# Two 32-row expert blocks per pass through the array instead of one, in a two-layer hybrid backbone with a grouped mixture of experts

## The reference

```python
D_MODEL, N_EXPERTS, TOP_K, EXPERT_FF = 1024, 16, 2, 512

def swiglu(x, wg, wu, wd):
    return (jax.nn.silu(x @ wg) * (x @ wu)) @ wd

def moe(v, router_w, router_bias, w_gate, w_up, w_down, s_gate, s_up, s_down):
    ...
    out = swiglu(xt, s_gate, s_up, s_down)
    for e in range(N_EXPERTS):
        out = out + gates[:, e:e + 1] * swiglu(xt, w_gate[e], w_up[e], w_down[e])
    return out.reshape(B, T, D)
```

## Time and profile before

| | |
|---|---|
| median of the three runs | 2375.11 us (2373.59 to 2384.86) |
| profiled execution, first to last instruction | 2369.5 us |
| profiled execution's own time | not listed apart; the median lies 5.6 us above its span |
| expert blocks of layer 0 | 772.1 to 1126.4 us, 354.3 us |
| expert blocks of layer 1 | 2059.8 to 2345.5 us, 285.7 us |
| TensorE matmul busy, whole span | 1976.5 us (83%) |
| DMA, mean over the span | 161 GB/s |

### The profile page before, as it was taken

One profiled execution on the slowest core, in us unless ns is written; L12 is line 12 of the kernel. 1 busy time (PEld: TensorE's weight loads), 2 busy tenths in 40 slices (PEclk: granted clock), 3 DMA queues, 4 the chain that ended last, 5 costly groups with the idle time before them and its releaser, 6 DMA issues. The chain is left out here.

```text
span 2369.5 us, 58411 instructions
## 1 busy us (share of the span) xinstructions
PE 1976.5 (83%) x26021; PEld 1357.2 (57%) x26021; DVE 951.9 (40%) x1675; ACT 701.9 (30%) x1524; POOL 331.0 (14%) x211
## 2 busy tenths in 40 slices
PE   6999998998989788889396897678888887967775
PEld 3777765446744344445243783678888855634333
DVE  3184244783051111111434774666676552211112
ACT  3234543763230000000314223545544222000001
POOL 1443400003310000000110541311122000000000
PEclk8999998998989899989698997899999978988888
DMA  8544525004374897977520300000000025999984
GB/s 301 196 178 167 189 107 200 14 1 142 108 274 165 312 340 269 343 250 273 164 97 27 107 27 1 3 4 4 4 4 4 4 92 173 323 381 348 343 316 177
DMA packets 184017, 381.14 MB, mean 161 GB/s; under 512 B 14394, under 2 KB 43670, under 8 KB 183510
## 3 DMA queue, kind: packets, MB, share of 16 engines
q1 hardware_dynamic: 165216, 343.82, 40.7%
q10 hardware_dynamic: 15094, 20.99, 2.9%
q0 software_dynamic: 3456, 12.58, 1.4%
HBM read 634.54 MB, written 25.95 MB: 279 GB/s over the span
## 5 line engine op out<-in xcount | busy, mean ns | idle before, releaser
L1810 PE MATMUL banks<-arena 128*32 128x256 f32 x1696 | 234.1, 424 | 94.6 <-DMA arena<-in_exp_w_up_dram 94.6
L369 PE MATMUL banks<-parts 128*128 128x512 f32 (+1 forms) x1096 | 243.9, 375 | 22.1 <-DVE parts L383 11.3
L1811 PE MATMUL banks<-arena 128*32 128x256 f32 x1696 | 234.1, 424 | 0.0
L369 PEld LDWEIGHTS banks<-parts 128*128 128x128 f32 x1096 | 195.2, 193 | 59.4 <-DVE parts L383 11.5
L1810 PEld LDWEIGHTS banks<-arena 128*32 128x32 f32 x1696 | 105.5, 120 | 184.4 <-DMA arena<-in_exp_w_up_dram 102.9
L377 DVE TENSOR_TENSOR arena<-banks,arena 64x256 f32<-64x256 f32 (+3 forms) x128 | 65.5, 512 | 339.3 <-ACT arena L1876 244.5
L2559 PE MATMUL banks<-arena 64*64 64x64 f32 x4224 | 159.5, 225 | 49.5 <-DVE arena L380 19.2
L1876 ACT ACTIVATE arena<-banks 64x256 f32<-64x256 f32 x78 | 29.7, 381 | 573.3 <-PE banks L1811 573.3
L2559 PEld LDWEIGHTS banks<-arena 64*64 64x64 f32 x4224 | 148.2, 140 | 53.0 <-DVE arena L380 20.5
L2559 PE MATMUL banks<-ring 64*64 64x64 f32 x4224 | 159.2, 225 | 8.0 <-issue 7.8
L369 PE MATMUL banks<-arena,ring 128*128 128x256 f32 (+1 forms) x528 | 156.5, 459 | 8.5 <-PEq L316 8.5
(11 more groups left out here) (368 smaller groups left out, 3601.9 us busy)
## 6 DMA issues: line engine op xcount, KB each, us to landing
arena<-in_exp_w_gate_dram SPq DMA_DIRECT2D x106, 1024.0 KB
arena<-in_exp_w_up_dram SPq DMA_DIRECT2D x106, 1024.0 KB
arena<-in_exp_w_down_dram SPq DMA_DIRECT2D x53, 2048.0 KB
ring<-in_exp_w_gate_dram SPq DMA_DIRECT2D x50, 1024.0 KB
ring<-in_exp_w_up_dram SPq DMA_DIRECT2D x50, 1024.0 KB
ring<-in_exp_w_down_dram SPq DMA_DIRECT2D x25, 2048.0 KB
ring<-in_w_mod_dram SPq DMA_DIRECT2D x24, 2048.0 KB, 9.1
ring<-in_ab_w_in_dram SPq DMA_DIRECT2D x10, 2048.0 KB, 13.9
```

Source lines behind the costliest of these rows:

```text
L369: m = nc.tensor.matmul(o, a, b, start=first and n == 0, stop=last and n == len(pairs) - 1)
L1810: nc.tensor.matmul(o[r:r + BLOCK, 0:256], x, up[:, k, c], start=k == 0, stop=k == KD - 1)
L1811: m = nc.tensor.matmul(o[64 + r:64 + r + BLOCK, 0:256], x, gate[:, k, c], start=k == 0, stop=k == KD - 1)
```

## The change

The step of the engines becomes a pair of blocks, g = (2g, 2g+1); the last pair of each layer has one block, since 47 and 31 are odd. The four column groups of `gate_up` now hold up and gate of two blocks, 512 columns wide, and those of `down` the two halves of two blocks. Silu, multiply and copies take both blocks at once. SyncE still walks through single blocks in its old order, but what it waits for are the labels of pairs. There are still three places for weights.

```diff
-                    sp.wait_ge(*at(("first half", i - 3)))
+                    sp.wait_ge(*at(("first half", (i - 3) // 2)))
                     load_half(i, 0, expert, cond=new)
-                    sp.wait_ge(*at(("gate up", i - 3)))
+                    sp.wait_ge(*at(("gate up", (i - 3) // 2)))
                     load_half(i, 1, expert, cond=new)
                     if i > 3:
-                        sp.wait_ge(*at(("down", i - 4)))
+                        sp.wait_ge(*at(("down", (i - 4) // 2)))
                         load_down(i - 1, before, cond=before_new)
...
-                for i in range(nb + 1):
-                    if i < nb:
-                        gate_up(i, 0)
...
+                for g in range(ng + 1):
+                    if g < ng:
+                        gate_up(g, 0)
+                    if g > 0:
+                        turn_hidden(g - 1)
+                    if g < ng:
+                        gate_up(g, 1)
+                    if g + 1 < ng:
+                        turn_x(g + 1)
+                    if g > 0:
+                        down(g - 1)
...
-                pe.wait_ge(half_landed[part][p], 32 * (w0[p] + i // 3 + 1))
+                for i in blocks_of(g):
+                    pe.wait_ge(half_landed[part][i % 3], 32 * (w0[i % 3] + i // 3 + 1))
...
                 for k in range(4 * part, 4 * part + 4):
+                    for i in blocks_of(g):
+                        side = i % 2
+                        x = m_xt[:, g % 2, k, BLOCK * side:BLOCK * side + BLOCK]
+                        for first_row, w in ((0, expert_weights(i % 3, 1)), (64, expert_weights(i % 3, 0))):
+                            r = first_row + BLOCK * side
+                            m = nc.tensor.matmul(o[r:r + BLOCK, :], x, w[:, k, :], start=k == 0, stop=k == KD - 1)
...
 # down
+                for k in range(4):
+                    for i in blocks_of(g):
+                        x = m_th[:, g % 2, k, BLOCK * (i % 2):BLOCK * (i % 2) + BLOCK]
+                        for half in range(2):
+                            r = 64 * (i % 2) + BLOCK * half
+                            m = nc.tensor.matmul(ps[3 + g % 2][r:r + BLOCK, :], x, expert_weights(i % 3, 2)[:, k, 512 * half:512 * half + 512],
+                                                 start=k == 0, stop=k == 3)
```

More of the change, by code:

```diff
@@ L1593, in moe_block @@
             ng = (nb + 1) // 2
[L1594 to L1595 removed]
+            x0, w0, stored_before = x_pairs_before[0], list(loads_before), list(stores_before)
             x_pairs_before[0] += ng
@@ L1598, in moe_block, with blocks_of @@
                 loads_before[p] += in_place[p]
+            def blocks_of(g):
+                return range(2 * g, min(2 * g + 2, nb))
+            for g in range(ng):
+                stores_before[g % 2] += 16 * len(blocks_of(g))
+            stored_after = list(stores_before)
             def block_of(i):
@@ L1806, in gate_up @@
                 for k in range(4 * part, 4 * part + 4):
[L1807 to L1811, removed]
@@ L1812, in gate_up @@
-                m.then_inc(pe_done, pe.tick(("gate up" if part else "first half", i)))
-            def turn_hidden(i):
-                pe.wait_ge(*at(("hidden", i)))
-                pe.wait_ge(*at(("shared out", 2 * nt - 1)))
[L1817 to L1820, removed]
@@ new lines, in gate_up, with turn_hidden @@
+                m.then_inc(pe_done, pe.tick(("gate up" if part else "first half", g)))
+            def turn_hidden(g):
+                r = BLOCK * len(blocks_of(g))
+                pe.wait_ge(*at(("hidden", g)))
+                pe.wait_ge(*at(("shared out", 2 * nt - 1)))
+                pe.wait_ge(*at(("hidden out", g - 1)))
+                for c in range(4):
+                    m = nc.tensor.transpose(ps[2][:, c * 64:c * 64 + r], m_hid[0:r, c * P:(c + 1) * P], ident[0:r, 0:r])
+                m.then_inc(pe_done, pe.tick(("hidden turned", g)))
@@ new lines, in down @@
+            def down(g):
+                pe.wait_ge(*at(("hidden out", g)))
+                pe.wait_ge(*at(("y out", g - 2)))
+                for i in blocks_of(g):
+                    pe.wait_ge(down_landed[i % 3], 16 * (w0[i % 3] + i // 3 + 1))
+                for k in range(4):
+                    for i in blocks_of(g):
+                        x = m_th[:, g % 2, k, BLOCK * (i % 2):BLOCK * (i % 2) + BLOCK]
[3 more added lines that the diff above has]
+                                                 start=k == 0, stop=k == 3)
+                m.then_inc(pe_done, pe.tick(("down", g)))
@@ L1869, in act_ @@
                 load_x(2)
[L1870 to L1883, removed]
+                for g in range(ng + 2):
+                    if g >= 2:
+                        store_y(g - 2)
+                    if g < ng:
+                        r = BLOCK * len(blocks_of(g))
+                        act.wait_ge(*at(("gate up", g)))
+                        act.wait_ge(*at(("hidden", g - 1)))
+                        nc.scalar.activation(m_sil[0:r, :], ps[g % 2][64:64 + r, :], ACT.Silu).then_inc(act_done, act.tick(("silu", g)))
+                    if g + 1 < ng:
+                        x_out(g + 1)
+                        if g + 3 < ng:
+                            load_x(g + 3)
+                    if l == 1 and g - 1 in turns_at:
+                        j = turns_at.index(g - 1)
                         act.wait_ge(*at(("h turned", j)))
@@ L1986, in dve_ @@
                     nc.vector.tensor_copy(m_ysh[:, d // 2, 512 * (d % 2):512 * (d % 2) + 512], ps[2 + d % 5]).then_inc(dve_done, dve.tick(("shared out", d)))
[L1987 to L2001, removed]
@@ new lines, in dve_ @@
+                for g in range(ng + 1):
+                    if g > 0:
+                        dve.wait_ge(*at(("hidden turned", g - 1)))
+                        dve.wait_ge(*at(("down", g - 3)))
+                        r = BLOCK * len(blocks_of(g - 1))
+                        nc.vector.tensor_copy(m_th[:, (g - 1) % 2, :, 0:r], ps[2][:, 0:256].rearrange("p (c t) -> p c t", c=4)[:, :, 0:r]).then_inc(
+                            dve_done, dve.tick(("hidden out", g - 1)))
+                    if g < ng:
+                        r = BLOCK * len(blocks_of(g))
+                        dve.wait_ge(*at(("silu", g)))
+                        dve.wait_ge(*at(("hidden turned", g - 1)))
+                        vmul(m_hid[0:r, :], ps[g % 2][0:r, :], m_sil[0:r, :]).then_inc(dve_done, dve.tick(("hidden", g)))
+                    if g > 0:
+                        r = 64 * len(blocks_of(g - 1))
+                        dve.wait_ge(*at(("down", g - 1)))
+                        if g >= 3:
+                            dve.wait_ge(y_stored[(g - 1) % 2], stored_before[(g - 1) % 2] + 32 * (g // 2 - (g % 2 == 0)))
+                        nc.vector.tensor_copy(m_yout[0:r, (g - 1) % 2, :], ps[3 + (g - 1) % 2][0:r, :]).then_inc(dve_done, dve.tick(("y out", g - 1)))
```

62 lines of the change are left out of this document (21 added, 41 removed).

## The result

The changed kernel takes **2556.02 us** (median of 4 runs, 2552.03 to 2558.84) against 2374.45 us before: ratio 1.0767, 95% interval 1.0736 to 1.0797, so 182 us slower. Slower was right; 2470 us was 86 us short, and the time lies above the range.

A forecast was written before the change was run, and what follows sets the result against it. Neither TensorE nor DMA was the whole bound; what decided was how early loads are issued against when TensorE wants them. Waits and half clock added 69 us in layer 0 and 26 in layer 1: 2375.1 + 95 = 2470 us, range 2430 to 2520.

The forecast's parts named there:

- An odd load ... 9.1 us as median: Expert stretches: odd block's first half issued 1.7 us late, then 9.1 us to land, 10.8 us waited in all.
- Second halves: Expert stretches: waits for second weight halves, mostly behind odd loads, 2 us each or 0.8 where DMA's queue is full.
- Even loads are hidden: Expert stretches: even blocks' loads are issued one pair, 13.7 us, ahead, so they stay hidden as before.
- Nothing else moved by more than 2: Windows outside the two layers' expert stretches: none moves by more than 2 us.
- A bubble without any load, 2.0 us: Pairs without loads: TensorE waits 2.0 us for SyncE's skipped loads, most of it two register reads.
- A real down load in front, 3.0: SyncE before a pair's first half: issuing a real down load adds 1.1 us to the bubble, 3.0 in all.
- The clock ... 1.7 per wait: TensorE behind each wait of 2.8 us or more: half clock costs 1.7 us more; none behind 2.0 us bubbles.
- Rival 1: TensorE's clock falls at each bubble too: +26 to +40 us, 2500 us; chance 0.20.
- The matmuls gain: nothing: TensorE's expert matmuls: time follows columns, not the number of matmuls, so pairing blocks gains zero.
- rival 3: Gate and up are bound by the array's issue: at 50 ns saved per record, 2280 us; chance 0.03.
- rival 4: 512-column matmuls in four groups run one after another, each half four times as long: hundreds of us more; chance 0.01.
- Rival 2: SyncE's order does not bind, so loads hide better: 2350 or less in full, 2410 in half; chance 0.07.

The follow-up runs named there:

- e3: Changed kernel with y stores spread over 16 DMA engines and SyncE issuing the next blocks' gate and up loads before its wait for down: 2358.02 us.

## Why the prediction was wrong, point by point

The waits of the changed kernel, by kind, against the terms of the sum, with the same kernel with spread stores (e1) beside them. Each is the sum of TensorE's gaps over what they are without waits:

| us | predicted | changed | stores spread |
|---|---|---|---|
| layer 0: six odd loads | 74.6 | 102.6 | 75.8 |
| other pairs' first waits | 37 | 39.7 | 33.9 |
| second halves | 12 | 15.0 | 4.9 |
| half clock | 19 | 27.9 | 17.8 |
| layer 1: five odd loads | 77.4 | 98.3 | 75.6 |
| other pairs' first waits | 20 | 25.0 | 16.7 |
| second halves | 8 | 11.5 | 8.0 |
| half clock | 15 | 18.8 | 13.0 |

One row of the second halves in the changed kernel, pair 14, whose even block loads:

```profile
1057.96 0.62 PE L1818 MATMUL banks<-arena 128*32 128x512 f32 x2 [3.61 <-DMA arena<-in_exp_w_up_dram]
```

- **The step that failed: "An odd load ... 9.1 us as median".** In the changed kernel the first half of the odd load of step 19 took 13.8 us from its issue, and the wait before it was 15.5 us where 10.8 had been forecast; the eleven odd loads together waited 200.9 us, not 152. The forecast price came from single loads, which land in other parts of the program, with no store beside them, and what the stores take came in as q10's 8.6% of the DMA engines, a mean over 16. The change halved the engines a store runs on and doubled the size of the rows on each, and puts both stores of a pair right before the odd load. With the stores spread, all four terms of odd loads and first waits are right within 4 us each, the stretches' DMA shares are the 0.7 and 0.85 foreseen (0.72 and 0.86), and the stretches, 413.8 and 303.9 us, are nearer to my 423 and 311 than those of the changed kernel are. The time of that kernel, 2442, is 28 below 2470; the prediction had, in effect, priced it.
- **Part of that agreement is luck.** With the stores spread, the single odd loads of pairs 4 and 9 waited 10.4 and 10.6 us, much as forecast. Pairs 7 and 18, and pair 12 of layer 1, were priced the same, 10.8, although their even block loads too (steps 14, 36 and 24); they waited 13.2, 12.8 and 14.8 us. Pair 1 and those priced at 15.6 and 16.9 came out 1.0 to 2.2 lower, which makes up for it.
- **"Second halves": right number, wrong place.** Of the 12 and 8 forecast, 18 stood behind odd loads. In the changed kernel none of the eleven odd loads has a wait before its second half; the 15.0 and 11.5 us all stand in pairs whose even block alone loads (pairs 12, 14, 15, 21, 23; 2, 5, 8, 15 of layer 1). Only load 4's, forecast 2, was meant so; it was 1.5.
- **"Even loads are hidden" failed the same way.** In the changed kernel pairs whose even block alone loads wait 17.6 us before first halves in layer 0 and 13.7 in layer 1, where the same pairs without loads have 9.2 and 5.1. Second halves of even blocks are late too (3.6 us in pair 14). With spread stores the former are 11.8 and 5.3, about a bubble each, the second halves 4.9 and 8.0. The sign "next to none before pairs whose even block alone loads" was wrong as well: the bubble stands there too, as the sum itself had it.
- **"Nothing else moved by more than 2" was wrong by 10 us.** The last y store lands 6.2 us behind its issue (3.2 before), and behind layer 0, where y is gathered, TensorE waits 34.0 us (L1760) against 28.1. With spread stores that is 26.4. It is the same cause.
- **"A bubble without any load, 2.0 us": right,** 1.9. "A real down load in front, 3.0": 2.2. The order on SyncE costs what the steps say: 98 us come back when it alone is mended, and 70.8 us of bubbles exist without loads.
- **"The clock ... 1.7 per wait": too low.** Behind the wait of 15.5 us in pair 9 the first half takes 6.34 us, not 3.6: the granted clock was 0.57 for all of it. Behind the wait of 3.2 us in pair 12 it is the 1.7 taken from the earlier trace rows, 5.3 us. The six odd loads of layer 0 cost 1.7 to 2.9 us each, the five of layer 1 1.3 to 2.7, and not in the order of their waits. The five pairs behind an odd load, priced in, waited 2.2 us and kept 1.00; late even loads took their place. Rival 1 did not come in the changed kernel, whose bubbles of 1.6 to 2.6 us before first halves all kept 1.00, but it isn't refuted: three bubbles in two other runs did not (2.21 and 2.58 us with the stores spread, 2.27 without loads).
- **"The matmuls gain: nothing": right,** 471.4 and 471.1 us without loads. So rival 3 (issue-bound) is out, and with it the estimate of 94 us gained; rival 4 too. Down takes 3.6 us as written.
- **Rival 2 (loads hide better)** was wrong for the changed kernel. Its reckoning, 2350 if SyncE's order did not bind, is what e3 gives, 2358, but there the stores had to be mended as well.

What I ought to have done: the diff changes `q=4` into `q=2` in the store's view. I costed the store by bytes and by issues, which do not change, and never asked on how many engines it runs. The rule on engines stands in the Trainium skill, in the section named above, and the trace of before holds the counts to see it: four semaphore writes a store.

## What to carry to other kernels

Ask of every DMA, however small, how many engines it runs on: here the outermost dimension of the store's view decided it. Two stores of 128 KB on two engines made a load land 4.8 us later while their queue showed a share of 4 to 8%. Its signs here were a mean DMA share of 0.63 with TensorE waiting for DMA, and a tail of 55 GB/s at the end of a load. Spreading one store gave 41 us to a kernel that no one had asked about it. And where work is made coarser with the same number of buffers, count the lead of each load again, and look for a wait in the issuing queue that now stands in front of it.

The fastest of these versions is the kernel before with its store on 16 engines, 2328.70 us; the pairs, with stores and order mended, reach 2358.02.

## What the runs showed of the hardware

- Rows of 2 KB took 93 ns on two engines and 101 on sixteen (means of layer 0's stores), rows of 1 KB 48 to 50 ns on two, four and sixteen. The spread stores make 32 semaphore writes a block instead of 2 (64 instead of 4 in the kernel before), of some 10 ns each, and cost nothing that shows.
- The granted clock: 0.57 for the 6.3 us behind a wait of 15.5 us, 1.00 behind bubbles of 1.9, and either behind bubbles of 2.2 to 2.6 us (1.00 in the changed kernel, 0.68 twice with its stores spread).
- Two register reads on SyncE put 1.1 to 1.2 us on TensorE's path at each pair where they stood ahead of a load, none where something hid them.
